# An attention stage: local and compressed value products moved into the next pass, weighing joined, memory exponentials moved up

## The reference, cut to what matters

```python
s = einsum(q, k_cmp) - slope * dist;  p_c = masked_softmax(s);  o_c = p_c @ v_cmp     # compressed keys, 31
s = einsum(q, k_slc) - slope * dist;  p_s = masked_softmax(s);  o_s = p_s @ v_slc     # selected keys
s = einsum(q, k_win) - slope * dist;  p_w = masked_softmax(s);  o_w = p_w @ v_win     # local (window) keys
out = g0 * o_c + g1 * o_s + g2 * o_w
m = softmax(einsum(mq, mem_k)) @ mem_v                                                # memory, 4 heads, 256 keys
```

## Time and profile before

| | |
|---|---|
| median of 3 runs | 2027.15 us (2026.88 to 2027.37) |
| profiled execution | 2027.15 us, span 2025.4 us |
| TensorE busy | 1950.2 us, 96% |
| VectorE busy | 1122.7 us, 55% |
| ScalarE busy | 736.2 us, 36% |
| GpSimd busy | 180.3 us, 9% |
| mean granted TensorE clock | 0.986 |
| the stage of the change | 757.4 to 867.2 us |

### The profile page before, as it was taken

The page is one execution under the profiler, slowest core; times in us unless marked ns, Lnnn a source line. Parts: engine busy times, 40 slices in busy tenths (PEclk is TensorE's granted clock), DMA queues, the critical chain, the costliest instruction groups (busy, mean ns, idle before and its releaser), DMA issues. The chain is left out here.

```text
span 2025.4 us, 27255 instructions
## 1 busy us (share of the span) xinstructions
PE 1950.2 (96%) x10481; PEld 1590.7 (79%) x10481; DVE 1122.7 (55%) x1628; ACT 736.2 (36%) x1150; POOL 180.3 (9%) x178
## 2 busy tenths in 40 slices
PE   7999999999999998999999999999989999999998
PEld 7788688888788876578888788888777688888786
DVE  6435456556535547736655633667554467777532
ACT  7442542222334436624222232435433342222323
POOL 2201020000002004401000000200231020000001
PEclk9999999999999999999999999999998999999999
DMA  6311123332323520023233233322100223323221
GB/s 234 125 45 43 58 89 93 104 95 91 104 94 89 147 62 1 1 84 115 84 107 100 83 104 93 95 70 87 42 2 2 74 83 102 106 83 103 94 83 42
DMA packets 135495, 167.73 MB, mean 83 GB/s; under 512 B 28354, under 2 KB 102631, under 8 KB 135399
## 3 DMA queue, kind: packets, MB, share of 16 engines
q1 hardware_dynamic: 135219, 166.37, 26.6%
q10 hardware_dynamic: 180, 0.05, 0.0%
HBM read 164.29 MB, written 2.10 MB: 82 GB/s over the span
## 5 line engine op out<-in xcount | busy, mean ns | idle before, releaser
L195 PE MATMUL bank<-h_hi,w_hi 128*128 128x512 f32 x2192 | 861.2, 393 | 23.2 <-DVE h_lo L423 6.8
L196 PE MATMUL bank<-h_lo,w_hi 128*128 128x512 f32 x2192 | 856.3, 391 | 0.0
L197 PE MATMUL bank<-h_hi,w_lo 128*128 128x512 f32 x2192 | 856.0, 390 | 0.0
L142 DVE TENSOR_TENSOR w_lo<-raw,w_hi 128x1024 fp32r<-128x1024 f32 x274 | 334.6, 1236 | 582.3 <-ACT w_hi L136 581.8
L195 PEld LDWEIGHTS bank<-h_hi,w_hi 128*128 128x128 f32 x2192 | 413.4, 189 | 118.8 <-issue 13.0
L136 ACT CAST w_hi<-raw 128x1024 fp32r<-128x1024 f32 x274 | 284.4, 1047 | 597.8 <-PE bank L195 586.9
L197 PEld LDWEIGHTS bank<-h_hi,w_lo 128*128 128x128 f32 x2192 | 413.5, 189 | 87.0
L196 PEld LDWEIGHTS bank<-h_lo,w_hi 128*128 128x128 f32 x2192 | 413.3, 189 | 85.8 <-issue 1.4
L1501 ACT ACTIVATE scratch<-scratch 128x512 f32<-128x512 f32 x66 | 41.8, 633 | 250.2 <-DVE scratch L1565 250.2
L323 POOL TENSOR_TENSOR tail<-keep 128x512 f32<-128x512 f32 x7 | 9.6, 1377 | 1233.8 <-ACT keep L307 1216.8
L1564 DVE SCALAR_TENSOR_TENSOR scratch<-keep,vecs,scratch 128x512 f32<-128x512 f32 x88 | 66.2, 752 | 10.2 <-DVE scratch L1563 1.2
(11 more groups left out here) (464 smaller groups left out, 1867.3 us busy)
## 6 DMA issues: line engine op xcount, KB each, us to landing
raw<-in_w_up SPq DMA_DIRECT2D x176, 256.0 KB, 3.0
raw<-in_w_down SPq DMA_DIRECT2D x44, 512.0 KB, 3.2
raw<-in_w_ffn_up SPq DMA_DIRECT2D x88, 256.0 KB, 3.3
raw<-in_w_mix_in SPq DMA_DIRECT2D x24, 512.0 KB, 3.8
raw<-in_w_ffn_down SPq DMA_DIRECT2D x22, 512.0 KB, 3.4
raw<-in_w_mem_kv SPq DMA_DIRECT2D x16, 512.0 KB, 5.0
raw<-in_a_w_in SPq DMA_DIRECT2D x16, 512.0 KB, 3.7
raw<-in_a_w_out SPq DMA_DIRECT2D x8, 512.0 KB, 4.6
```

The lines of the kernel that those rows point to most:

```text
L142: dve.tensor_tensor(k.w_lo[n % RING][:, :], k.raw[n % RING][:, :], k.w_hi[n % RING][:, :].bitcast(F32), ALU.subtract)\
L195: a = pe.matmul(out, sh, mh, start=first, stop=False)
L196: pe.matmul(out, sh, ml, start=False, stop=False)
L197: c = pe.matmul(out, sl, mh, start=False, stop=last)
```

## The change

Nothing is added or removed; instructions change places in three engines' lists.

- TensorE: the local values of pass j - 1 are done in pass j, row 0 behind turn 0, row 1 behind turn 1, rows 2 and 3 and the compressed values behind turn 2; the memory values of pass j - 1 go from turn 1 to turn 3. For pass 3 they all follow the last turn.
- VectorE: `weigh_sel` does both halves in one piece at turn 10, behind the memory lows; `coef_cmp` goes from turn 12 to turn 11.
- ScalarE: the memory exponentials go from turn 11 to turn 9; `finish` and `finish_mem` both stand at turn 4 (before: 1 and 3).

```diff
--- before.py
+++ after.py
@@ -2042,17 +2042,19 @@
                     turn(j, m)
                     if j < 3 and m < NB:
                         scores(NB * (j + 1) + m)
-                    if j >= 1 and m == 1:
+                    if j >= 1 and m < 2:
+                        values_local(j - 1, (m,))
+                    elif j >= 1 and m == 2:
+                        values_local(j - 1, (2, 3))
+                        values_cmp(j - 1)
+                    elif j >= 1 and m == 3:
                         values_mem(j - 1)
                     elif m in (6, 7):
                         values_sel(j, (m - 6,))
                     elif m == 8:
                         values_sel(j, (2, 3))
-                    elif m == 11:
-                        values_local(j, (0, 1))
-                    elif m == 12:
-                        values_local(j, (2, 3))
-                        values_cmp(j)
+            values_local(3, (0, 1, 2, 3))
+            values_cmp(3)
             values_mem(3)
 
         def copy_turned(copy, eng, j, m):
@@ -2107,13 +2109,13 @@
                 L(dve.reciprocal(coef[j][br][:, :, :], tot[j][br][:, :, :]))
                 return dve.tensor_tensor(coef[j][br][:, :, :], coef[j][br][:, :, :], gate(j, b), ALU.mult)
 
-            def weigh_sel(j, a):
-                if a == 0:
-                    dve.wait_ge(e_done, 16 * j + 16)
-                    L(coefficients(j, 0, 1))
-                for i in range(4):
-                    p = block(j, 0, a, i)
-                    dve.tensor_scalar(p, p, col(coef[j][0], i, a), None, ALU.mult).then_inc(p0_ready, 1)
+            def weigh_sel(j):
+                dve.wait_ge(e_done, 16 * j + 16)
+                L(coefficients(j, 0, 1))
+                for a in range(2):
+                    for i in range(4):
+                        p = block(j, 0, a, i)
+                        dve.tensor_scalar(p, p, col(coef[j][0], i, a), None, ALU.mult).then_inc(p0_ready, 1)
 
             def coef_local(j):
                 dve.wait_ge(e_done, 16 * j + 8)
@@ -2133,8 +2135,7 @@
                 lows(n)
                 if n == 5:
                     coef_local(0)
-            weigh_sel(0, 0)
-            weigh_sel(0, 1)
+            weigh_sel(0)
             coef_cmp(0)
             coef_mem(0)
             value = lambda kk: k.catT[:, kk, :]
@@ -2143,16 +2144,15 @@
                     if (NT * j + m) % 2 == 1:
                         copy_turned(dve.tensor_copy, dve, j, m).then_inc(t_dve, 1)
                     if j < 3:
-                        if m == 9:
-                            weigh_sel(j + 1, 0)
                         if m < NB:
                             lows(NB * (j + 1) + m)
                         if m == 6:
                             coef_local(j + 1)
+                        if m == 10:
+                            weigh_sel(j + 1)
                         if m == 11:
-                            weigh_sel(j + 1, 1)
+                            coef_cmp(j + 1)
                         if m == 12:
-                            coef_cmp(j + 1)
                             coef_mem(j + 1)
                     elif m == 7:
                         dve.wait_ge(t_full, NT * 3 + 5)
@@ -2217,13 +2217,10 @@
                 for m in range(NT):
                     if (NT * j + m) % 2 == 0:
                         copy_turned(act.copy, act, j, m).then_inc(t_act, 1)
-                    if j < 3 and m < 9:
+                    if j < 3 and m < NB:
                         exps(NB * (j + 1) + m)
-                    if j < 3 and m == 11:
-                        exps(NB * (j + 1) + 9)
-                    if j >= 1 and m == 1:
+                    if j >= 1 and m == 4:
                         finish(j - 1)
-                    if j >= 1 and m == 3:
                         finish_mem(j - 1)
                     if j == 3 and m == 4:
                         act.wait_ge(t_full, NT * 2 + 10)
```

## The result

The changed kernel takes 2040.88 us (median of 4 runs, 2040.0 to 2042.28) against 2027.26 us (2026.88 to 2027.42): ratio 1.0066, 95% interval 1.0054 to 1.0079. It is 13.6 us slower; 12.2 were forecast. When the profile is read, keep in mind that the profiled execution took 2042.77 us, 1.9 us more than the median; these four runs lie 2.3 us apart where those of the kernel before lie 0.5 us apart. In all 25 executions of the changed kernel on record the time is 2038.55 to 2042.77 us.

The account below looks back on a forecast made before the run. TensorE was taken to bound the stage. Idle of 3.56 + 2.9 + 3.56 less 1.16 and 0.27 gave +8.6 us, the clock +3.6, together +12.2 on 2027.15: 2039.4 us, range 2034 to 2046.

Parts of the forecast that it names:

- What bounds the stage: Edited stage, 773 to 866 us: TensorE bounds it; better cover could save no more than 3.7 us.
- Passes 0 and 2: Changes of pass behind 0 and 2: TensorE idles 3.11 us ahead of turn 12, 0.45 ahead of turn 0, 3.56 each.
- the upper bound of +0.7 us: VectorE's weighing in passes 0 and 2: extra time if it runs as slowly as beside GpSimd's scaling.
- Pass 1: Change of pass behind 1: TensorE idles 1.28, 1.22 and 0.38 us ahead of turns 12, 0 and 1, sum 2.9.
- What is given back: Later passes: the 1.16 us wait ahead of turn 6 of pass 2 goes; pass 3 waits 2.3 us against 2.57.
- Sum at full clock: Whole stage: added idle less what the moved work saves, +8.6 us before any fall of TensorE's clock.
- The clock: TensorE behind the 3.1 us idles of passes 0 and 2: half clock costs 1.8 us twice, +3.6; bounds 0 and 6.3.
- the rival with three falls: All three changes of pass: clock falls each time, 6.3 us, plus 1.4 for contended weighing; +16.3, 2043.5 us; chance 0.16.
- the clock holds: Rival, changes of pass: idle comes as worked out but the granted clock stays at 1.00; 2035.8 us; chance 0.17.
- Not slower: Rival, turns 0 to 6: deferred work is better cover there; at best 2023.4 us, likely 2025.7; chance 0.06.
- the weaker loss: Rival, changes of pass: TensorE finds half of the chain done; 2031 us; chance 0.06.
- The transposes: Pass 1's change, only transposes on TensorE: if they don't count as busy, the clock drops there too, some 2.1 us more.

Follow-up runs that it names:

- the kernel with filled waits: Changed kernel plus unread 128x512 matmuls ahead of turn 12 of passes 0 to 2 and turn 0 of pass 2: 2033.48 us against 2025.89, ratio 1.0039.
- the third filler: Two more unread matmuls ending the stage before, in the original kernel with two fillers, memory values and casts reordered: 2018.58 us against 2026.17, ratio 0.9952.

## Why the prediction was right, by its steps

**What bounds the stage.** TensorE, and only its waits and its clock could move the time. Right: all engines' work stayed, 14.7 of the profiled execution's 15.6 us stand on the ruler, and there in TensorE's brackets and record lengths.

**Passes 0 and 2.** Turn 12 was put at 797.35 with E at 793.27, E + 4.08; it came at E + 3.96. Turn 0 was put at E + 5.08 and came at E + 5.04. The weighing took 2.37 us from 795.39 to 797.76, as from the uncontended row (2.36). GpSimd's scaling (L2170) ended at 795.57, 0.2 us into it, so the upper bound of +0.7 us did not come.

**Pass 1.** Turn 12 at E + 2.13 (2.25), turn 0 at E + 4.08 (4.06). The third wait, 0.38 ahead of turn 1, shows no bracket, since at half clock TensorE came later; with the waits filled it was 0.26.

**What is given back.** The 1.16 us ahead of turn 6 of pass 2 went. Pass 3 waits 0.44, 1.53 and 0.33, together 2.30; 2.3 were forecast.

**Sum at full clock.** 8.6 us were forecast; the kernel with filled waits shows 8.5 on the ruler and 7.6 in the medians.

**The clock: the term that was mis-sized.** It was 3.6 us, two falls at 1.8. On the ruler it is 86.6 - 80.4 = 6.2 us, by the medians 6.0, and there are three falls. Set beside the kernel with filled waits, stretch by stretch, they cost 2.5, 1.2 and 2.4 us (E of pass 0 to E of pass 1 30.1 against 27.6; E of pass 1 to E of pass 2 28.2 against 27.0; E of pass 2 to the last memory values 28.3 against 25.9). Two things were off. Pass 1's waits of 1.09 and 1.29, which I counted as harmless from rows at 1.16 and 1.45, were followed by half clock, both here and with the exponentials moved back. And the falls behind the long waits cost 2.5 where I had taken 1.8 from two rows: the first lasted from about 797.3 to 804.2, the third from about 855.4 to 862.1. So the course was that of the rival with three falls, whose 6.3 us for the clock were right; only its 1.4 for a contended weighing did not come. The median fell among the times of my own forecast, 2037 to 2041.5, and that is in part luck: the profiled execution, 2042.77, lies above them.

**The rivals.** That the clock holds is out (0.50 in the table). Not slower and the weaker loss are out: the waits are as long as the chain worked out. Moving the order back shows that it isn't one part: values alone +6.3, weighing with exponentials +2.9 on the ruler, exponentials alone +13.6, the falls of the clock included.

**The transposes.** The Trainium skill's rule ("TensorE: Matmul & The Clock Gate", Part 4: PE-mode transpose) that they don't count as busy in the way matmuls do would have had pass 1's clock fall, and it fell. That alone does not decide for the rule, since pass 1 also holds 2.4 us of waiting. Against it stand 850 to 854 of the kernel before, at 1.00 with little but turns, and the kernel with only the values moved: in pass 0 TensorE had nothing but turns from E to E + 4.3, with 2.06 us of waits among them, in pass 1 nothing but turns from E to E + 3.7 with a wait of 1.66, and the clock was 1.00 through and behind both. In its pass 2 the same order and the same waits as in pass 0 were followed by half clock. So turns alone don't bring the clock down here; whether they count for less is not shown.

## What to carry to other kernels

Work moved out of a gap must be replaced by something, or the chain that it covered is bare: list, from the last result on which the chain hangs, what each engine does until the next one can go on, before and after. An engine that is half idle can still cost microseconds if one instruction that waits is put ahead of a copy that others need; look at what stands behind the waiting instruction, not at the busy share. And price a wait of TensorE by its length and by the clock behind it: here the clock added 6.2 us to 8.5. Last, look for a gain of 1 us in a stretch of the trace: the third filler's 1.3 us does not show in times that lie 6 us apart.

## What the runs showed of the hardware

- The clock fell behind waits far shorter than the 2.97 and 3.89 us of the earlier trace rows: behind 1.09 + 1.29 us (changed kernel), 1.10 + 0.96 (exponentials back), 0.23 + 1.83 (values only, pass 2). It did not fall behind the same 0.23 + 1.83 in pass 0 of that same execution, nor behind 1.66 in its pass 1, nor behind 1.28 alone. The length of a wait does not settle it. The Trainium skill, "TensorE: Matmul & The Clock Gate", Why this matters for your kernels, advises against idle gaps of TensorE between bursts of matmuls; here two short ones, 1.09 and 1.29 us with one turn between them, were followed by half clock.
- Unread 128x512 matmuls in a wait of TensorE held the granted clock at 1.00 in every place where they were tried, in the stage and ahead of it, and took nothing from the work behind: turn 0 at E + 5.05 with them, E + 5.04 without.
- A fall of the clock has no fixed price. On the traces here one cost 1.2 to 4.7 us, and behind equal waits it differed too: 4.7 and 3.3 us behind the two of 2.80 with only the exponentials moved, nothing and an estimated 1.5 behind the two pairs of 0.23 + 1.83 with only the values moved. One execution does not tell what the next will pay.
